# Attention with key tiles of 16, 128 and 128: the leading keys of two heads turned in one transpose, and their values as block-diagonal tiles

## What is computed

```python
def one_block(args):                      # a block of 128 queries, all keys
    i, qi = args[0], args[1]
    s = jnp.einsum('bqhd,bkhd->bhqk', qi, k) * scale
    if decay is not None:
        s = s + args[2][..., None] - ck[:, :, None, :]
    mask = (kpos[None, :] <= qpos[:, None]) & kvalid[None, :]
    s = jnp.where(mask[None, None], s, NEG)
    p = jax.nn.softmax(s, axis=-1)
    return jnp.einsum('bhqk,bkhd->bqhd', p, v)

for i in range(DEPTH):                    # DEPTH = 4
    mix = (fox_mixer, swa_mixer, mla_mixer)[i % 3](h, ...)
    h = layer_norm(DEEPNORM_ALPHA * h + mix, ln1_g[i], ln1_b[i])
    ffn = conv_glu_ffn(h, ffn_w_in[i], ffn_conv_w[i], ffn_conv_b[i], ffn_w_out[i], valid)
    h = layer_norm(DEEPNORM_ALPHA * h + ffn, ln2_g[i], ln2_b[i])
```

## Time and profile before

| | |
|---|---|
| median of three runs | 1455.12 us (1454.45 to 1457.86) |
| the profiled execution | 1464.82 us |
| its span, first to last instruction | 1463.0 us |
| mean granted TensorE clock in it | 0.968 |
| TensorE, matmuls in flight | 1375.1 us, 94% of the span |
| VectorE, ScalarE, GpSimd busy | 66%, 56%, 17% |
| chain that ended last | TensorE 78%, VectorE 11%, ScalarE 8% |

### The profile page before, as it was taken

How to read it: one execution, slowest core, us unless ns; L and a number is a source line. 1 busy time by engine, 2 the same in 40 slices (tenths; PEclk the granted TensorE clock), 3 DMA queues, 4 the chain that set the end, 5 groups by cost and what they waited for, 6 DMA issues and landing times.

```text
span 1463.0 us, 30534 instructions
## 1 busy us (share of the span) xinstructions
PE 1375.1 (94%) x10517; PEld 1304.4 (89%) x10517; DVE 960.2 (66%) x2024; ACT 823.8 (56%) x1653; POOL 243.5 (17%) x219
## 2 busy tenths in 40 slices
PE   7899999999888999999976999999998999999997
PEld 7788999999876999999965799999997888999996
DVE  4665777765587577765585857777555665777754
ACT  4565576654555576654643647666455555766644
POOL 2000034420000034330010002443001000144400
PEclk9899999999998999999997999999999899999999
DMA  7232355556321345555341134555633332355562
GB/s 267 88 100 74 116 164 186 178 180 196 108 68 44 116 143 187 172 183 191 102 133 40 59 116 129 186 173 173 201 116 116 100 103 85 119 185 188 184 208 81
DMA packets 56933, 203.37 MB, mean 139 GB/s; under 512 B 6256, under 2 KB 8336, under 8 KB 56720
## 3 DMA queue, kind: packets, MB, share of 16 engines
q1 hardware_dynamic: 56784, 202.20, 43.5%
q0 software_dynamic: 64, 0.03, 0.0%
HBM read 201.13 MB, written 1.05 MB: 138 GB/s over the span
## 4 chain that ended last, share of the span: by engine, by line
PE 78%; DVE 11%; ACT 8%; issue 3%; DMA 0%; ACTq 0%; DVEq 0%
PE ps L374 22%; PE ps L377 21%; PE ps L378 21%; PE ps L458 3%; PE ps L487 3%; DVE w_lo L1097 2%; PE ps L505 2%; ACT w_hi L736 2%; ACT probs L786 2%; ACT h L850 2%; DVE h L1237 1%; DVE h_lo L1231 1%; PE ps L394 1%; PE ps L397 1%; PE ps L398 1%
## 5 line engine op out<-in xcount | busy, mean ns | idle before, releaser
L1097 DVE TENSOR_TENSOR w_lo<-raw,w_hi 128x1024 fp32r<-128x1024 f32 x378 | 461.8, 1223 | 276.1 <-ACT w_hi L736 274.9
L374 PE MATMUL ps<-h_hi,w_hi 128*128 128x272 f32 (+1 forms) x1752 | 516.0, 295 | 11.7 <-DVE w_lo L1097 7.5
L378 PE MATMUL ps<-h_hi,w_lo 128*128 128x272 f32 (+1 forms) x1752 | 507.7, 290 | 0.0
L377 PE MATMUL ps<-h_lo,w_hi 128*128 128x272 f32 (+1 forms) x1752 | 507.4, 290 | 0.0
L736 ACT ACTIVATE w_hi<-raw 128x1024 fp32r<-128x1024 f32 x378 | 396.3, 1050 | 172.5 <-PE ps L374 158.5
L374 PEld LDWEIGHTS ps<-h_hi,w_hi 128*128 128x128 f32 x1752 | 335.8, 192 | 15.0 <-issue 9.3
L377 PEld LDWEIGHTS ps<-h_lo,w_hi 128*128 128x128 f32 x1752 | 335.8, 192 | 1.2
L378 PEld LDWEIGHTS ps<-h_hi,w_lo 128*128 128x128 f32 x1752 | 335.2, 191 | 0.0
L374 PE MATMUL ps<-hid_hi,w_hi 128*128 128x272 f32 (+2 forms) x644 | 187.8, 292 | 4.6 <-DVE keys L1097 1.6
L1071 POOL TENSOR_TENSOR gated<-y 128x272 f32<-128x272 f32 x88 | 138.4, 1573 | 286.3 <-DVE y L1469 286.3
L377 PE MATMUL ps<-hid_lo,w_hi 128*128 128x272 f32 (+2 forms) x644 | 185.5, 288 | 0.0
(11 more groups left out here) (150 smaller groups left out, 1902.1 us busy)
## 6 DMA issues: line engine op xcount, KB each, us to landing
raw<-in_weights SPq DMA_DIRECT2D x378, 512.0 KB, 3.7
cst<-in_consts SPq DMA_DIRECT2D x1, 1787.5 KB, 11.7
h<-in_x SPq DMA_DIRECT2D x2, 544.0 KB, 5.4
out<-h SPq DMA_DIRECT2D x8, 128.0 KB, 1.8
keys<-y POOLq DMA_DIRECT2D x2, 17.0 KB, 2.1
```

The costliest lines, as they stand in the source:

```text
L374: m = pe.matmul(b, whi, xhi, start=n == 0, stop=False)
L377: pe.matmul(b, whi, xlo, start=False, stop=False)
L378: m = pe.matmul(b, wlo, xhi, start=False, stop=n == len(tiles) - 1)
L1097: return dve.tensor_tensor(out_, a_, b_, op)
```

## The change

The keys are now tiled like the queries, 16, 128 and 128. For each head three full transposes turn the second and third key tiles (128 queries by keys 16 to 143, and the last 128 queries by keys 16 to 143 and 144 to 271). The probabilities of the 16 leading keys of *both* heads are put beside each other by `normalise` in a new buffer `meta`, in groups of 32 columns, and turned by one full transpose for each of two query chunks together, with a 16-row one for the first 16 queries. So `turn_pair` has 3 + 3 + 2 transposes for a pair in place of 12, and counts `transposed` three times a pair.

The matmuls of the 16 leading keys then serve both heads at once: they read value tiles z1 and z2 (`v_tok[:, 0:2]`) that are block-diagonal, each head's 16 keys in its own 32 rows and its own 64 columns, with 128 output rows. The other two tiles go by head as before. To make the block-diagonal tiles, ScalarE's new `spread_value` copies the first 32 tokens of a value panel twice, by half, into the zeroed `v_spare`, and `turn_value` transposes that too, so that it has four transposes and a wait on a new semaphore `v_spread`. `copy_value` and `copy_turned` are of one piece for each bank. `ROW` goes from 320 to 288.

```diff
-ROW = 320
+ROW = 288
-PCOL = (0, P, 3 * P)
+PROW = N_META + P
+PCOL = (0, PROW, 2 * PROW)
...
             def turn_value(m, where):
                 b = ps[:, where]
-                for ch in (2, 0, 1):
-                    a, e = ch * P, min(T, (ch + 1) * P)
-                    t = pe.transpose(b[0:e - a, ch * P:(ch + 1) * P], v_t(m)[:, a:e], ident)
-                t.then_inc(v_turned, 1)
+                pe.transpose(b[:, 2 * P:3 * P], v_t(m)[:, N_META:N_META + P], ident)
+                pe.transpose(b[:, 3 * P:4 * P], v_t(m)[:, N_META + P:T], ident)
+                pe.wait_ge(v_spread, n_spread[0] + 1)
+                n_spread[0] += 1
+                pe.transpose(b[:, 0:P], v_spare[:, m % 2, 0:P], ident)
+                pe.transpose(b[:, P:2 * P], v_spare[:, m % 2, P:2 * P], ident).then_inc(v_turned, 1)
...
-                one(PT1 + TAIL - P, 1, P)
-                one(PTW - P, 2, 2 * P, TAIL)
-                one(0, 0, 0)
-                one(N_META, 1, 0)
-                one(N_META + P, 2, 0)
-                one(PT1 + TAIL, 2, P).then_inc(transposed, 1)
+                def head(s):
+                    pr, b = probs[:, r0 + s], ps[:, 4 + s]
+                    pe.wait_ge(normed, h0 + s + 1)
+                    if m:
+                        pe.wait_ge(pt_copied, h0 + s - 1)
+                    k1 = PCOL[2] + N_META
+                    pe.transpose(b[:, 0:P], pr[:, PCOL[1] + N_META:PCOL[2]], ident)
+                    pe.transpose(b[:, P:2 * P], pr[:, k1:k1 + P], ident)
+                    return pe.transpose(b[:, PT2:PTM], pr[:, k1 + P:PW], ident)
+                head(0).then_inc(transposed, 1)
+                head(1)
+                pe.transpose(ps[:, 5, PTM:PTW], meta[:, m % 2, 2 * GROUP:], ident).then_inc(transposed, 1)
+                pe.transpose(ps[:, 4, PTM:PTM + N_META], meta[0:N_META, m % 2, 0:P],
+                             ident[0:N_META, 0:N_META]).then_inc(transposed, 1)
...
             def mix(a, kind, m):
+                pe.matmul(ps[:, 6, q1:q2], z1, turned, start=True, stop=False)
+                pe.matmul(ps[:, 6, q2:T], z2, turned, start=False, stop=False)
+                pe.matmul(ps[:, 6, 0:q1], z1, first, start=False, stop=False)
+                for n, (lo, c0, c1) in enumerate(((q1, 0, PT2), (q2, PT2, PTM))):
                     for s in range(2):
...
+            def spread_value(m, panel):
+                act.wait_ge(bank_free, panel + 1)
+                if n_spread[0] >= 2:
+                    act.wait_ge(v_turned, n_spread[0] - 1)
+                n_spread[0] += 1
+                spare = v_spare[:, m % 2].rearrange("p (c n) -> p c n", c=2)
+                for s in range(2):
+                    rows = slice(HD * s, HD * s + HD)
+                    ins = act.activation(spare[rows, :, GROUP * s:GROUP * s + GROUP],
+                                         v_t(m)[rows, 0:GROUP].unsqueeze(1).broadcast_to([HD, 2, GROUP]), ACT.Copy)
+                ins.then_inc(v_spread, 1)
...
+                first = probs[:, hn % 4, 0:3 * PROW].rearrange("p (c n) -> p c n", c=3)[:, :, 0:N_META]
+                group = meta[:, hn // 2 % 2].rearrange("p (c n) -> p c n", c=3)
+                for ch in (1, 2):
+                    pr = probs[:, hn % 4, PCOL[ch] + N_META:PCOL[ch] + CHUNKS[ch][1]]
+                    dve.tensor_scalar(pr, pr, rinv[:, s, ch:ch + 1], None, ALU.mult)
+                tt(group[:, :, GROUP * s:GROUP * s + N_META], first,
+                   rinv[:, s, :].unsqueeze(2).broadcast_to([P, 3, N_META]), ALU.mult).then_inc(normed, 1)
```

More of the change, by code:

```diff
@@ L212, in build_program @@
         probs_t = sb("probs_t", [P, 2, PTW])
+        meta = sb("meta", [P, 2, 3 * 2 * GROUP])
+        v_spare = sb("v_spare", [P, 2, 3 * P])
         stats = sb("stats", [P, 2, 3, 3])
@@ L500, in mix @@
                 pe.wait_ge(o_split, PAIRS * a + m)
-                for n, (t, lo, c0) in enumerate(((0, 0, 0), (1, P, PT1), (2, 2 * P, PT2))):
+                (_, q1), (_, q2) = CHUNKS[0:2]
+                pair = m // 4 if kind == "swa" else m
+                z1, z2 = (v_tok[:, n, pair * P:pair * P + P] for n in range(2))
+                turned, first = probs_t[:, 1, PTM:PTW], probs_t[:, 0, PTM:PTM + N_META]
+                pe.matmul(ps[:, 6, q1:q2], z1, turned, start=True, stop=False)
+                pe.matmul(ps[:, 6, q2:T], z2, turned, start=False, stop=False)
+                pe.matmul(ps[:, 6, 0:q1], z1, first, start=False, stop=False)
+                for n, (lo, c0, c1) in enumerate(((q1, 0, PT2), (q2, PT2, PTM))):
                     for s in range(2):
-                        hn = 2 * m + s
-                        col = (hn // 8 if kind == "swa" else hn) * HD
-                        ins = pe.matmul(ps[HD * s:HD * s + HD, 6, lo:T], v_tok[:, t, col:col + HD],
-                                        probs_t[:, s, c0:c0 + T - lo], start=n == 0, stop=n == 2)
+                        col = 2 * P + m // 4 * HD if kind == "swa" else (2 * m + s) * HD
+                        ins = pe.matmul(ps[HD * s:HD * s + HD, 6, lo:T], v_tok[:, 2 + n, col:col + HD],
+                                        probs_t[:, s, c0:c1], start=False, stop=n == 1)
                 ins.then_inc(mixed, 1)
@@ L583, in _ @@
                         if m >= 2:
-                            turn(a, 2 * m - 4)
-                            turn(a, 2 * m - 3)
+                            turn_pair(a, m - 2)
                         if m < PAIRS:
@@ L602, in swap, with turn_shared @@
                         n_swap[0] += 1
+                    def turn_shared():
+                        pe.transpose(ps[:, 5, 0:P], v_t(1)[:, N_META:N_META + P], ident)
+                        pe.transpose(ps[:, 5, P:2 * P], v_t(1)[:, N_META + P:T], ident)
+                        pe.wait_ge(v_spread, n_spread[0] + 1)
+                        n_spread[0] += 1
+                        for g in range(2):
+                            for z in range(2):
+                                ins = pe.transpose(ps[:, 4, (2 * g + z) * P:(2 * g + z + 1) * P],
+                                                   v_spare[:, g, z * P:z * P + P], ident)
+                        ins.then_inc(v_turned, 1)
                     base = n_swap[0] + 1
@@ L714, in o_ready @@
                     if k == 2:
-                        turn(a, HEADS - 2)
-                        turn(a, HEADS - 1)
+                        turn_pair(a, PAIRS - 1)
                     if k == 5:
@@ L913, in _, with spread_shared, copy_shared @@
                 elif kind == "swa":
+                    def spread_shared(panel):
+                        act.wait_ge(bank_free, panel + 1)
+                        act.wait_ge(v_turned, n_spread[0])
+                        n_spread[0] += 1
+                        for g in range(2):
+                            spare = v_spare[:, g].rearrange("p (c n) -> p c n", c=2)
+                            for s in range(2):
+                                ins = act.activation(
+                                    spare[HD * s:HD * s + HD, :, GROUP * s:GROUP * s + GROUP],
+                                    v_t(1)[HD * g:HD * g + HD, 0:GROUP].unsqueeze(1).broadcast_to([HD, 2, GROUP]),
+                                    ACT.Copy)
+                        ins.then_inc(v_spread, 1)
+                    def copy_shared():
+                        act.wait_ge(v_turned, n_v[0] + 1)
+                        act.activation(v_tok[:, 0:2, 0:2 * P].rearrange("p z (g n) -> p z g n", g=2),
+                                       ps[:, 4].rearrange("p (g z n) -> p z g n", g=2, z=2), ACT.Copy)
+                        act.activation(v_tok[:, 2:4, 2 * P:3 * P],
+                                       ps[:, 5, 0:2 * P].rearrange("p (c n) -> p c n", c=2),
+                                       ACT.Copy).then_inc(v_copied, 1)
                     gemm(a, "vk")
@@ L1028, in _ @@
             pool.memset(eps[:, 3:4], RMS_EPS * SCALE["mla"] ** -2).then_inc(init_done, 1)
-            for buf, value in ((stats, 1.0), (v_tok, 0.0), (probs_t, 0.0), (probs, 0.0)):
+            for buf, value in ((stats, 1.0), (probs, 0.0), (meta, 0.0), (v_spare, 0.0)):
                 pool.memset(buf[:], value).then_inc(init_done, 1)
```

81 lines of the change are left out of this document (35 added, 46 removed).

## The result

| | before | with the change |
|---|---|---|
| median | 1456.5 us (8 runs, 1451.6 to 1463.8) | 1469.7 us (8 runs, 1466.7 to 1472.0) |
| ratio, 95% interval | | 1.0075 (1.0050 to 1.0101) |
| the profiled execution, its span | 1464.8, 1463.0 | 1471.3, 1469.5 |
| mean granted clock of single executions | 0.967 to 0.977 (24 of the first set below) | 0.967 to 0.970 |

What follows compares the result with a forecast made beforehand. TensorE was busiest (94% of the span); attention stages were judged by which wait ends last. Terms -4.8 + 3.05 + 1.96 + 4.0 + 0.1 = +4.3, plus 1.5 for the clock, gave +5.8 on 1455.1: 1461 us, range 1452 to 1468.

Steps and rivals of the forecast that it cites:

- Turning: TensorE's transposes of a pair's probabilities: 1.04 us after against 1.63, 0.6 saved per pair (bounds 0.44 and 0.75).
- Mix: TensorE's matmuls of probabilities with values: 0.38 us more per pair, bounds 0.3 and 0.55.
- Fox passes: Full passes over a head pair in the two fox layers: 0.4 us less each, -4.8 in all; passes of 10.5.
- Value tiles: Four full transposes in place of three: +0.19 us for each of 24 value panels; ScalarE's two spread copies 0.39.
- Value 0 of layer 0: First value panel of the layer 0 fox stage: TensorE goes on at 18.45 instead of 16.35, +2.1 us.
- Mla passes: Passes over a head pair in the mla layer: 8.8 us against 7.88, with TensorE's longest wait ended by `v_spare`.
- The rival by which mla falls to the lower clock: New mla passes idle about 1.1 us, bringing 3.4 us at the lower level in four passes: 1467 us; chance 0.18.
- Swa: Swa layer's passes: ScalarE's shorter copies give 0.06 us a pass, -0.36 in all.
- Tails: Ends of the four attention stages: lose what the mix costs, gain what turning saves, worse at the lower clock: +0.45 us.
- Clock: Lower TensorE clock behind the new wait at value 0, idle 1.9 us in mid stage: +1.5 us, added once.
- The rival by which the clock makes the change faster: Late values 6 and 7 cut the idling before fox's first scores, whose first passes keep full clock: 1449 us; chance 0.08.
- Row stride: Row length of the split activations, packing tiles closer: costed at nothing; if it matters, every panel moves and the forecast is void.

Runs made afterwards that it cites:

- the first set below: First of four sets of timings in which follow-up kernels ran beside the unchanged kernel before, whose own median there was 1454.7 us.
- the two filled versions: Changed kernel with useless identity products in TensorE's tail waits in fox and swa, 41 or 11 in all: 1458.7 us (ratio 1.0004) and 1459.1 us (1.0019).
- the filled version: Changed kernel with useless identity products ahead of waiting tail mixes, 9 in each fox layer, 12 and 11 in swa: 1458.7 us, ratio 1.0004.
- early spreads: Changed kernel with ScalarE's `v_spare` fills moved earlier, in mla ahead of the first head's exponentials: 1466.9 us, ratio 1.0074.

## Why the prediction fell short

- *Turning:* 1.01 us where I had 1.04. Right in the passes. In the tails I booked it as a gain as well (-0.3 in mla, and part of the +0.45). There ScalarE's copy ends last, so that nothing is gained, and the idle time grows by what was saved.
- *Mix:* +0.54 against 0.93 in mla before (825.50 to 826.43), where I had +0.38 and a bound of 0.55. I counted the 16 columns at 0.85 ns each, 0.03 us; they take 0.22. Each pass loads its own weights, and the loads of these passes also start every 0.11 us, whatever the columns; which of the two sets the pace was not tried.
- *Fox passes:* 10.64, not 10.5. The mis-sized mix is the reason, since TensorE, not the keys, now ends last. Ten full passes gave -2.8.
- *Value tiles:* +0.11 each (27.85 to 28.21 in the trace, 0.36 against 0.25), where I had 0.19, as four transposes follow the same pattern as three. The spread took 0.50, not 0.39.
- *Value 0 of layer 0:* +2.26 at the full clock, where I had +2.1. The first scores came 2.9 and 2.6 us later in the two filled versions, where I had 3.05, and 5.9 in the profile of the changed kernel, where the lower clock took 2.3 at this place alone (5.37 us for the panel at 19.02, in place of 3.10 in the filled version), against my 1.5. The values behind the gate were late and covered, as I said.
- *Mla passes:* 9.15, not 8.8, and by the steps of the sum: scores to exponentials 2.26 (2.25), exponentials 1.21 (1.2), copies 0.86 (0.86), the second head 1.20 (1.2), spread to TensorE 0.56 (0.44), two transposes 0.27 (0.22), mix 1.47 (1.3), panel 1.32 (1.3). The chain was right link by link. The rival by which mla falls to the lower clock did not come true: from 806 to 846 the granted clock is 1.00, though TensorE idles 1.08 us in every pass.
- *Swa:* passes of 7.75 against 7.80, as forecast.
- *Tails:* +5.6 us where I had +0.15. **This is the step that failed:** I put the tails at the balance of mix and turning, and left out the clock behind their waits. I looked for the lower clock only where the change adds a wait, and not where an old wait grows because TensorE arrives sooner. I had the row for it, the 1.70 us wait with the clock of 0.88 behind it.
- *Clock:* +1.5 once. With the waits of three tails filled the tails took 10.5 us less. The rival by which the clock makes the change faster was true in part: in layer 3 the first passes took 4.6 us less, and my theory of -11 us for early spreads failed on that: mending one wait made another whole, and the tails stayed. That rival also misread its row: the wait of 0.99 us at 1100.97 is followed by the lower clock, since the granted clock of 1096 to 1107 is 0.84.
- *Row stride:* not nothing, it seems, but 0.6 us in most MLP stages.

Still open: why the clock falls behind a wait of 1.75 us in one trace and not in another, where the 7 us lie by which the medians differ more than the two traces, and the stride.

## To carry to other kernels

When an edit makes TensorE faster ahead of a wait that another engine ends, cost the wait as well: the saved time is idle time there, and the lower clock behind it can cost more than the edit saves in all other passes (here +5.6 us in the tails against -2.8 in ten fox passes). Move needed work into such waits first, and compare kernels by several executions and their granted clocks, since two profiled executions of one kernel differed here by as much as the edit moved. A step added to a full queue should stand where that engine was idle anyway, not directly ahead of its user.

## What the hardware showed that I had not expected

- Work that serves nothing made the kernel faster: 41 products of 0.25 us, 10 us of TensorE's time in three layers, placed where it idled, and the time fell by 11 us. The kernel before already does so in its layer norms, with 280 products at L529, 37.6 us of TensorE.
- A matmul pass of 16 columns behind others of 128 output rows takes 0.11 us from start to start, as a pass of 128 columns does (0.11), and one of 144 takes 0.12.
- One program, the kernel before, took 1463.6 us at a mean granted clock of 0.969 and 1451.7 at 0.976, in executions of the same set; behind the same wait of 1.75 us in layer 3 the clock fell in both traces of it and stayed in that of the version with the other stride.
